# A head's probabilities stored and read back before the unit's load on SyncE, with the weight units of those slots split three ahead

## The reference, cut to what matters

```
q_a, f_a, i_a, g_a, q_b, k_b, v_b, f_b, gates = split(h @ w_in)
o_a = rmsnorm(hgrn2_chunkwise(q_a, f_a, i_a)) * silu(g_a)      # the recurrence's output
o_b = fox_attention(q_b, k_b, v_b, f_b)                        # 8 heads of 128
#   s = q.k/sqrt(dh) + c[t] - c[s];  p = softmax(s);  o = p @ v
y = gate0 * (o_a @ w_branch_a) + gate1 * (o_b @ w_branch_b)
```

## Time and profile before

| | us |
|---|---|
| median of three executions | 1053.22 (1053.19 to 1053.32) |
| the profiled execution | 1055.78 |
| its span, first to last instruction | 1054.0 |
| TensorE busy in it | 1044.4 |
| VectorE busy | 756.2 |
| ScalarE busy | 598.8 |

### The profile page before, as it was taken

One profiled execution on the slowest core, in us unless ns is written; L12 is line 12 of the kernel. 1 busy time (PEld: TensorE's weight loads), 2 busy tenths in 40 slices (PEclk: granted clock), 3 DMA queues, 4 the chain that ended last, 5 costly groups with the idle time before them and its releaser, 6 DMA issues.

```text
span 1054.0 us, 12947 instructions
## 1 busy us (share of the span) xinstructions
PE 1044.4 (99%) x4939; PEld 872.2 (83%) x4939; DVE 756.2 (72%) x901; ACT 598.8 (57%) x800; POOL 73.2 (7%) x59
## 2 busy tenths in 40 slices
PE   9999999999999999999999999999999999999997
PEld 7888888888888888888888888788879988888886
DVE  5768778885787675468988978868778666867642
ACT  6573767764384645447784644554366657565531
POOL 1200000000000000000535500000000000000000
PEclk9999999999999999999999999999999999999999
DMA  9945899985487777557866845889875346777751
GB/s 363 393 129 170 297 291 304 306 261 196 176 278 239 248 224 237 190 203 257 255 192 212 240 160 182 266 275 309 304 261 187 117 165 206 240 241 233 247 163 40
DMA packets 97645, 243.89 MB, mean 231 GB/s; under 512 B 15104, under 2 KB 41904, under 8 KB 97456
## 3 DMA queue, kind: packets, MB, share of 16 engines
q1 hardware_dynamic: 94016, 231.51, 67.8%
q0 software_dynamic: 3136, 11.23, 2.9%
q10 hardware_dynamic: 432, 0.33, 0.1%
HBM read 220.48 MB, written 22.54 MB: 231 GB/s over the span
## 4 chain that ended last, share of the span: by engine, by line
PE 89%; DVE 4%; DMA 3%; ACT 1%; SPq 1%; issue 1%; DVEq 0%; ACTq 0%
PE ps L820 21%; PE ps L822 21%; PE ps L821 21%; PE ps L857 5%; PE ps L859 5%; PE ps L858 5%; DMA y_turned<-y_blocked 2%; DVE rest L1964 1%; PE ps L954 1%; PE ps L1144 1%; PE ps L1253 1%; PE ps L1254 1%; PE ps L1255 1%; DMA mem_turned<-mk_blocked 1%; DMA fpT<-fp_turned 1%
## 5 line engine op out<-in xcount | busy, mean ns | idle before, releaser
L1964 DVE TENSOR_TENSOR rest<-raw,high 128x2048 fp32r<-128x2048 f32 x129 | 295.2, 2304 | 78.2 <-ACT high L1368 77.7
L820 PE MATMUL ps<-high,xt_high 128*128 128x512 f32 x824 | 324.4, 394 | 0.2 <-DVE rest L1964 0.2
L821 PE MATMUL ps<-rest,xt_high 128*128 128x512 f32 x824 | 320.8, 389 | 0.0
L822 PE MATMUL ps<-high,xt_rest 128*128 128x512 f32 x824 | 320.8, 389 | 0.0
L1368 ACT ACTIVATE high<-raw 128x2048 fp32r<-128x2048 f32 x129 | 244.5, 1911 | 74.1 <-DMA raw<-in_units_dram 73.9
L822 PEld LDWEIGHTS ps<-high,xt_rest 128*128 128x128 f32 x824 | 154.7, 188 | 32.5
L820 PEld LDWEIGHTS ps<-high,xt_high 128*128 128x128 f32 x824 | 154.8, 188 | 31.6 <-DVE rest L1964 0.6
L821 PEld LDWEIGHTS ps<-rest,xt_high 128*128 128x128 f32 x824 | 154.8, 188 | 31.1
L1969 DVE SCALAR_TENSOR_TENSOR rest<-raw,wgain,high 128x512 fp32r<-128x512 f32 x176 | 119.0, 746 | 35.5 <-ACT high L1372 35.5
L1372 ACT ACTIVATE high<-raw,wgain 128x512 fp32r<-128x512 f32 x176 | 110.8, 716 | 9.3 <-DMA raw<-in_units_dram 9.3
L1628 ACT ACTIVATE act<-ps,recips 128x256 f32<-128x256 f32 x44 | 18.4, 470 | 85.1 <-PE ps L822 85.0
(11 more groups left out here) (372 smaller groups left out, 1450.6 us busy)
## 6 DMA issues: line engine op xcount, KB each, us to landing
raw<-in_units_dram SPq DMA_DIRECT2D x350, 512.0 KB, 4.9
gv_turned<-gv_blocked SPq DMA_DIRECT2D x11, 512.0 KB, 6.1
gv_t<-gv_turned SPq DMA_DIRECT2D x44, 128.0 KB, 3.6
turned<-blocked SPq DMA_DIRECT2D x22, 256.0 KB, 5.3
hid_t<-turned SPq DMA_DIRECT2D x88, 64.0 KB, 4.2
fox_turned<-fqT SPq DMA_DIRECT2D x6, 512.0 KB, 3.1
raw<-in_units_dram SPq DMA_DIRECT2D x8, 256.0 KB, 4.7
fqT<-fox_turned SPq DMA_DIRECT2D x16, 128.0 KB, 4.6
```

The costliest lines, as they stand in the source:

```text
L820: pe.matmul(out, sh, wh, start=first, stop=False)
L821: pe.matmul(out, sh, wr, start=False, stop=False)
L822: mm = pe.matmul(out, sr, wh, start=False, stop=last)
L1964: vec.tensor_tensor(rest[:, slot, c], raw[:, slot, c], high[:, slot, c].bitcast(F32), ALU.subtract).then_inc(unit_rest, 1)
```

## The change

On SyncE `turn_probabilities(u)` is called first in `load(u)`, and it now deals with one head, u - 112: it waits for VectorE's transposition, issues the store, waits until that store has landed, issues the four reads, and only then the load of unit u follows. On ScalarE slots 26 to 35 split up to `80 + u + 3` and not `80 + u + 5`; on VectorE slots 9 to 35 do. Behind the loop both have units 118 and 119 left to split. VectorE waits for both stores of the recurrence's output, and not one, before it writes `gate1` over their source.

```diff
             def load(u):
 
+                turn_probabilities(u)
                 slot = u % SLOTS
...
                 turn_tokens(u)
-                turn_probabilities(u)
...
             def turn_probabilities(u):
 
-                h = u - UNIT["win2"] - 33
+                h = u - UNIT["win2"] - 32
                 if 0 <= h < HH:
+                    sync.wait_ge(fp_blocked, h + 1)
+                    sync.dma_start(fp_turned[h], fpT[:, h % 3, :]).then_inc(fp_stored, 16)
                     sync.wait_ge(fp_stored, 16 * (h + 1))
                     src = fp_turned[h].rearrange("(q i) (r e) -> r i q e", q=4, r=4)
                     for r in range(4):
                         sync.dma_start(...).then_inc(fp_landed[h % 3], 16)
-                h += 1
-                if 0 <= h < HH:
-                    sync.wait_ge(fp_blocked, h + 1)
-                    sync.dma_start(fp_turned[h], fpT[:, h % 3, :]).then_inc(fp_stored, 16)
...
             for u in range(36):                                          # ScalarE
-                split_to(UNIT["win2"] + u + 5)
+                split_to(UNIT["win2"] + u + (5 if u < 26 else 3))
...
                 if u != 5:                                               # VectorE
-                    split_to(UNIT["win2"] + u + (4 if 5 < u < 9 or 20 < u < 23 else 3 if 8 < u < 21 else 5))
+                    split_to(UNIT["win2"] + u + (5 if u < 5 else 4 if u < 9 else 3))
...
                         if g:
-                            vec.wait_ge(oa_turn[1][1], 16)
+                            vec.wait_ge(oa_turn[1][1], 16 * TT)
```

## The result

The changed kernel takes 1064.47 us (median of four, 1063.96 to 1065.02) against 1053.20 us before (median of four, 1052.67 to 1053.32): a ratio of 1.0105, 95% interval 1.0093 to 1.0117, so 11.3 us slower. Its profiled execution took 1064.38 us, with a span of 1062.6 us.

What follows compares the result with a forecast made beforehand. TensorE, busy 1044.4 of 1054.0 us, was taken as the bound; its waits for late heads, 1.8, 5.5 and 1.8 us, less 0.4, gave +8.7 us on 1053.2: 1061.9 us, range 1052.8 to 1066, own range 1056 to 1067.

Steps and rivals of the forecast that it cites:

- The base of the sum: Starting time 1053.2 us, from which TensorE's earlier wait of 0.4 us at head 2 was subtracted as a gain.
- VectorE's lead of 2 us: On VectorE, the later split lets head 0's maxima start about 2 us earlier: transposed at 638.2, not 640.4.
- The plain turn: SyncE's turn without the output: store landed 6.1 us after the load's start T, turn 7.9 us against TensorE's 6.1 to 7.1.
- rival 1: On SyncE's queue, the store doesn't wait for the load ahead, lands in 1.8 us: 1052.8 to 1053.2 us; chance 0.23 with milder mixtures.
- T + 8.0: On SyncE, behind the output's 512 KB store, a head's store lands 8.0 us after the load's start T; heads 3 and 5.
- T + 9.8: On SyncE, behind the output's reads, a head's store lands 9.8 us after the load's start T; heads 4 and 6.
- Heads 5, 6, 7 late by 1.8, 7.3, 9.1 us: At TensorE's products, cumulative lateness of the heads' reads, giving three waits of about 1.8, 5.5 and 1.8 us.
- before head 7's product, which waits for SyncE anyway: On TensorE, where time lost to a clock fall after the long wait would lie; no size added.
- What else comes late hides behind that.: Output's second tile, unit 117's load and VectorE's wait before `gate1` come late, but add nothing behind the heads' lateness.
- rival 2: On ScalarE, unit 116 or 118 is missing because loads start later; price 5 us, time 1058 us; chance 0.03.
- SyncE's waits for `fp_turned` grow from 8.7 to some 40 us: Sign of being right: on SyncE, waits for the heads' stores grow so, with landings of 5 us and more.
- The later splits at a price of 0: On ScalarE and VectorE, splitting three and not five ahead costs 0; if cover went, some 2.3 us per split.

Runs made afterwards that it cites:

- e1: The kernel before with only the later splits and the wait of `gate1`, SyncE's order as before: 1053.14 us, ratio 0.9998.
- e11: The changed kernel run again with the same code: 1066.07 us, ratio 1.0118.
- e2: The changed kernel with the splits of before, so SyncE's new order alone: 1074.51 us, ratio 1.0210.
- e3: The changed kernel with the store still ahead of the load, but the wait for its landing and the reads behind the load: 1053.19 us, ratio 1.0001.
- e9: The changed kernel with only the four reads moved behind the load, the wait for the landing left ahead of it: 1055.11 us, ratio 1.0021.
- e7: The kernel before with the new splits, SyncE's old order and a wait for the landing right behind each head's store: 1055.17 us, ratio 1.0017.
- e6: The changed kernel with a quarter of the data in the stores and reads of the recurrence's output: 1057.41 us, ratio 1.0037.
- e4: The changed kernel with the heads' stores issued by GpSimd, SyncE only waiting for them and reading: 1054.39 us, ratio 1.0009.
- e5: The changed kernel with GpSimd's load of `mem` started earlier, at 682.2 and not 708.3: 1066.28 us, ratio 1.0115.
- e10: The changed kernel with GpSimd's load of `mem` waiting for head 6's product, started at 699.8 and not 708.3: 1070.10 us, ratio 1.0161.

## Why the prediction was right, point by point

The forecast was 1061.9 us, own range 1056 to 1067; measured were 1064.5. Direction, place and mechanism held. The sum was 2.6 us too small. One term, used twice, was over-sized and made heads 6 and 7 some 2 us later than they are; a loss of 4.0 us behind the heads was missing. The two partly cancel, so that the forecast is nearer than its terms are, which is luck. The timelines of TensorE in e1 (span 1051.5) and after (1062.6) show it best, because both have the same splits and run within 0.25 us of each other up to 680 us. The product of head 5 starts 1.2 us later in after, head 6 5.3, head 7 7.2; the matmuls behind it are 7.3 us late, those behind the wait for `mt_rest` and its half clock 11.3, and the last ones 11.0.

- **The base of the sum.** The profiled execution of before is 2.5 us longer than e1's, though before and e1 have the same median. It loses 0.6 us in the first 7 us, 0.7 at head 2 and 1.1 near 774; the last two hold the 0.4 and 1.3 us of the earlier trace rows. I subtracted the 0.4 us as a gain, but e1 (0 at `fpT`, 0.3 at the unit) has the time of before without it. Those waits were that execution's own, and no gain.
- **VectorE's lead of 2 us, head 0 transposed at 638.2.** Right, and more: 637.2 (636.63 + 0.58).

```profile
636.63 0.58 DVE L2090 STREAM_TRANSPOSE fpT<-fp 128x384 f32<-128x384 f32 x1
```

- **The plain turn: store landed at T + 6.1.** Right: 6.3 at head 7 (697.23 to 703.54). Heads 1 and 2 have 5.8 and 5.9, for another reason: SyncE waited for VectorE's transposition, issued the stores when the load was partly through, and they landed in 2.0 and 3.0 us. I had said that VectorE is no longer what SyncE waits for, yet it waited for VectorE four times, 6.2 us in all; that the time came out the same there is luck. No store behind a load landed in rival 1's 1.8 us; the nearest, 2.0, was issued 3.8 us after the load's start. For an idle queue the estimate of 2.5 us, with which the prediction said that the idle store agrees, is 0.7 us above the 1.8 of the earlier trace rows.
- **T + 8.0 behind the output's store.** Right: 7.9 (656.82 to 664.73, head 3) and 7.9 (677.40 to 685.31, head 5).
- **T + 9.8 behind the output's reads.** Over-sized: 8.5 (667.11 to 675.63) and 8.4 (687.10 to 695.46), 1.3 and 1.4 us less. The output's reads land 5.1 to 5.6 us after issue (the first tile's below) where the slowest in the earlier trace rows had 7.2 and 8.6. This is the term that failed; I took it from rows that had a head's four reads queued behind the output's, and now those come ahead of the load.

```profile
DMA to landing us min/median/max: 5.1/5.3/5.6
```

- **Heads 5, 6, 7 late by 1.8, 7.3, 9.1 us.** They were late by 1.2, 5.3 and 7.2 us. Both turns with the output's reads, 2.7 us too long together, lie ahead of head 6's and head 7's landings and account for it, less some small terms of the other sign (0.2 in head 7's turn, TensorE's deadlines 0.7 us earlier without the loss at head 2).
- **That a fall of the clock loses time "before head 7's product, which waits for SyncE anyway".** Right. The forecast gave head 7 a wait of 1.8 us; measured are 0.25 us of waiting and, in the stretch from 698 to 702, half the clock, which cost some 1.6. The fall took the place of the wait.
- **"What else comes late hides behind that."** Wrong, and the largest error: 4.0 us of the loss lie behind the heads, 2.15 us at `mt_rest` and some 1.6 of half clock, which no wait absorbs there. The sum followed the units up to 118 and not unit 119, whose load stands behind head 7's turn: ScalarE waits 5.83 us for it, takes up `mem` 12.0 us late, and the store and read of `mem` end 2.15 us after TensorE wants them. It is rival 2 (ScalarE finds a unit missing), which had 0.03: one unit later than the rival looked, and on top of the forecast's waits, not in their place. `mem` itself also took 10.0 us to land, among the loads that SyncE makes up for, but nothing waited for it. e11 shows that this part of the loss takes another form in another execution: against e1 it is 7.0 us late behind head 7, 9.1 behind `mt_rest`, and 13.4 behind the 3.2 us at a weight unit and its half clock. How it divides isn't settled by these runs.
- **"SyncE's waits for `fp_turned` grow from 8.7 to some 40 us."** Over-sized: 27.4 us up to 700, 32.1 with the eighth store. The other signs hold: TensorE waits at heads 5, 6 and 7, longest at 6, the load of unit 118 starts at 697.23, and VectorE is waited for up to head 3 only. Landings of 5 us and more came from head 3 on.
- **The later splits at a price of 0.** Right by e1. That they are needed for the order of SyncE (e2: ten more microseconds) the prediction didn't see.

Of the rivals, the first (landing in 1.8 us) needs the store ahead of the load without a wait behind it: that is e3, and its time is the one that the rival gave. The prediction added up the whole loop, and the loop is the cause: the landing ahead of the load, the reads behind it, and the output's turns in the same queue. It had a term for each; what it gains to take one of them away, the runs show. With the reads moved the loss is 2 us (e9, and e7 in the old order), with most of the output's traffic gone 4 (e6), with the stores started earlier 1 (e4). These don't add up, because only what lies above TensorE's deadline counts: head 7 is within 0.7 us of its time when seven turns take some 54 us, costs 1.5 at 58.0, and everything from there on is paid.

## What to carry to other kernels

Of a serial round trip on the queue that also carries the weights, add up the whole loop (landing behind a load, issue of the reads, the other turns) against the pace of the engine that wants its product; the loss begins where the loop is longer, and taking any one part out of it took away most of the loss here (7 to 11 of 11 us). Issue the store early, but put the long load between the store and the wait for it. Follow also the first load behind the last serial turn: the engine that splits it may stand there before a later stage's work, with a deadline of its own. Before a transfer is moved earlier, look whether anything waits for it, and what it then shares the DMA engines with.

## What the hardware showed

- A store of 192 KB lands 1.8 us after issue with nothing ahead, 5.1 to 6.5 us right behind a load of 1 MB (and up to 512 KB of other turns) of the same issuer. Issued by GpSimd within 2.4 us of the start of SyncE's load it took 5.5 to 6.9 us: another queue did not make it faster. In a plain turn of three kernels (after, e7, e9) the store had landed 6.2 to 6.3 us after the load's start, whether it was issued 1.2 or 2.8 us behind that start.
- Four reads of 48 KB each landed after 1.9 us alone (changed kernel, head 7) and, in the median, after 5.7 (e5) and 6.6 us (e10) beside a transfer of 1 MB that another engine had issued.
- The granted clock fell to half with waits of TensorE of 2.03 (e6), 2.15, 3.08 (e5), 3.22 and 3.62 (e11), 3.41 (e10), 3.87, 5.39 (e5) and 6.40 us (e10), and held behind 1.78 (e11), 1.51 (e6) and 1.20 us. In a fall matmuls show 0.63 us where 0.40 us is usual, and start every 0.43 us and not every 0.23. A fall in the changed kernel and e11 cost 1.4 to 1.7 us, by how much later than in e1 the matmuls are behind it. TensorE in the changed kernel, start and duration, ahead of the second fall and in it:

```profile
748.75 0.39 PE L818 MATMUL ps<-high,mt_high 128*128 128x512 f32 x1
...
750.75 0.63 PE L818 MATMUL ps<-high,mt_high 128*128 128x512 f32 x1
```

- The changed kernel's executions scatter more (1062.1 to 1067.8 in eight) than those of before (1052.5 to 1056.0 in 69): that small differences of transfers are no longer hidden once deadlines are missed would explain it, but isn't shown.
